# One even mixer rearranged: mLSTM sample tokens on partitions, new states on row halves, convolution taps in two chains

## The chip, the cores and the metric

One core of one Trainium2 chip. The time is device microseconds (us) of one launch, median of three runs. Engines: PE (TensorE matmul), PEld (its weight load), DVE (VectorE), ACT (ScalarE), POOL (GpSimd), SP (SyncE, which only issues DMAs here).

## The reference, cut to what matters

Two transformer layers run over 512 prompt tokens and 8 sequences of 8 sample tokens (64 "samples"), 576 tokens in all, D = 1024. Layer 0 has the even mixer, which is all that the change touches:

```python
def even_mixer(hn, state, W, j):
    a_val, a_gate, q, k, v, o, gates = split(hn @ W['ev_w_in'])
    u = a_val * sigmoid(a_gate)                      # 512 channels
    c = causal depthwise conv(u, 31 taps) + bias     # samples start from a stored history
    a_out = silu(layer_norm(c))                      # mean and variance over the channels
    li, lf = input gate, log_sigmoid(forget gate)    # 4 heads
    h, C1, n1, m1 = mlstm_scan(q, k * 128**-0.5, v, li, lf, C0, n0, m0)
    mix = concat(a_out, sigmoid(o) * h) @ W['ev_w_out']

# mlstm_scan, per head: s = (q k^T) * exp(decay - m);  den = sum(s) + w_inter * (q n0)
#   h = (s v + w_inter * (q C0)) / max(|den|, exp(-m));  C1 = decay * C0 + (w_s * k)^T v
```

For the prompt the old state is zero; each of the 8 sample sequences has its own C0 (128 x 128) and n0 per head. Before and behind the mixer stand SwiGLU blocks, a gated projection, and a second layer with attention.

## The kernel before, in words

**Products.** Channels lie on partitions and the 576 tokens on the free axis. A weight product is three matmuls (`mm3`, L642 to L644): the weight block `wr` rounded to fp32r, its remainder `wl`, and the same two parts of the input. A tile of 128 output channels takes 8 k-blocks x 2 token halves x 3 = 48 matmuls. Weights come in blocks of 2048 columns, two tiles of the mixer's input products or four of its output product. For each block SP loads `raw`, ACT rounds it to `wr` (L1218), POOL subtracts to make `wl` (L581), and PE then takes it. There are two such slots. PE's output goes to two PSUM banks, in turn banks 0-1 and 2-3, and the tile after next may start once DVE has emptied them.

**Even mixer, first half.** The products run in the order `glu` (4 blocks, 8 tiles: value and gate of u), the gate rows (48 + 48 narrow matmuls), `kv` (4 blocks) and `qo` (4 blocks). Beside them:
- DVE makes u (`up` for the prompt, `us` for the samples, L1905, L1906), then the 31 taps of 4 channel groups, one group at a time (`conv_chunk`, L1866; the accumulator is PSUM bank 6). Each tap waits for the one before. Chunks of 8 taps stand between the evacuations of tiles: three in `glu`, six in `kv`, seven in `qo`.
- POOL makes the sample products `prod` (`sample_taps`, L597, 8 instructions a group), DVE sums them (`sum_taps`, L1895). There is one `prod` buffer, so group j waits for the sum of group j - 1. POOL's order in `kv` is block, group 0, block, group 1, and so on (L614 to L619).
- After the gate rows DVE runs the row chain for decay and maximum (L1915 to L1949), with the evacuation of the first `kv` tile in its midst (`kT`, L1735).
- PE turns K and V (`turn`, L758) between tiles; ACT copies them out (L1342, L1344).

**Even mixer, second half (the tail).** PE spreads the rows of maxima (L796), forms the sum for the layer norm mean (L885), then of squares (L892). Then come the heads: for each, five units of scores (L808) and values (L823, L825; the samples' at L828, L829); DVE multiplies scores by decays that ACT made (`weigh`, L1979; `Ds`, L1416, L1419). `former` (L843, L845) is the old state's part for the samples: 8 matmuls of 8 columns with C0 as weights and one for n0. The denominator goes ACT Abs, DVE max, ACT Ln, ACT Exp, DVE multiply (L1487, L2025, L1491, L1493, L2033); that last step releases `states` on PE: 4 matmuls for the prompt (L854) and 8 of 64 rows for the samples (L858). DVE then makes the new states (`new_states`, L2050, L2054). The output product of the conv half (8 tiles of 24 matmuls, "conv pieces") is dealt out between heads:

```python
CONV_PIECES = {0: ((), ()), 1: ((0,), (1,)), 2: ((2,), (3,)), 3: ((4,), (5, 6, 7))}   # (before, after the states)
```

The order of ACT in the tail is written out by hand (from L1422): the copies `Mb`, the squares, then for each head decays, `kw` (L1477), at heads 1 and 3 the rounding of a weight block, the denominator steps, `xr` (L1495); behind head 0's, `conv_silu` (L1462 to L1466). After the last piece the output product of the mLSTM half (`out_mlstm`) starts.

Of the kernel before, what the change touches and what calls it, by code (L numbers as in the profile page):

```python
# [23 lines left out]
P = 128  # L24
# [28 lines left out]
CONST = dict(ident=128, cm=128, neg_incl=128, sb_neg=128, blk_ml=64, blk_col=8,  # L53
# [69 lines left out]
def build(nc, A):  # L123
# [94 lines left out]
    gcol = sb("gcol", [P, 2 * ST * HEADS], at=z)  # L218
# [3 lines left out]
    kwm = sb("kwm", [SMP, NB, P], at=z)  # L222
    smp = sb("smp", [P, HEADS, 3, SMP], at=z)
    wsm = sb("wsm", [SMP, NB], at=z)
    qn = tiny
    ENDS = [z[0]]
    Pm = [tg, sg]
    z = [ZONE]
# [62 lines left out]
    CONV_PIECES = {0: ((), ()), 1: ((0,), (1,)), 2: ((2,), (3,)), 3: ((4,), (5, 6, 7))}  # L291

    def rows_bank(hh):

        return 6 + hh % 2

    def floor_bank(hh):

        return 7 - hh % 2

    def state_banks(hh):
        return (4, 5, 7) if hh == HEADS - 1 else (NUM, DEN, rows_bank(hh))
# [268 lines left out]
    def _(e):  # L571
# [66 lines left out]
    def _(e):  # L638
# [110 lines left out]
        def turn(src, phase, t, n, bank=4):  # L749
# [12 lines left out]
        def turn_kv(n):  # L762
            turn(kT[:, n, :] if n < 4 else vtmp[n - 4][:], "kv", n, n)
# [5 lines left out]
        def turn_cols():  # L769
# [3 lines left out]
            for q, row in enumerate((rowa, rowws)):  # L773
                for i in range(ST):
# [3 lines left out]
                                     C("ident", 0, 4, rows=4))  # L778
            mm.then_inc(S("cols_turned"), 1)

        def spread_samples():

            e.wait_ge(S("cols_copied"), 4)
            for hh in range(HEADS):
# [3 lines left out]

        gemm("qo", xin(1), None, lambda t: turn_kv(6 + t) if t < 2 else turn_cols() if t == 2 else
             spread_samples() if t == 3 else None)  # L790

        e.wait_ge(S("cols_copied"), 6)
        for hh in range(HEADS):
            if hh == 2:
                e.wait_ge(S("tile_evacuated"), evac_at("qo", 7))
            e.matmul(ps[:, (4, 5, 2, 3)[hh], :], sel(hh), rowM[:, 0:SEQ], start=True, stop=True  # L796
                     ).then_inc(S("rows_spread"), 1)

        def scores(k):
# [6 lines left out]
            else:  # L806
                e.wait_ge(S("max_copied"), k + 1)
# [3 lines left out]
        def values(k):  # L811
            hh, i = divmod(k, ST)
            rws = rows_bank(hh)
# [13 lines left out]
            else:  # L827
                e.matmul(ps[:, rws, 0:SMP], vn[0:SMP, i, hh, 0:P], pm[0:SMP, 0:SMP], start=True, stop=True)  # L828
                e.matmul(ps[:, rws, SMP:2 * SMP], ones[0:SMP, :], pm[0:SMP, 0:SMP], start=True, stop=True  # L829
                         ).then_inc(S("pv_done"), 1)  # L830

        def floor(hh):

            e.matmul(ps[:, floor_bank(hh), :], sel(hh), rowem[:, 0:SEQ], start=True, stop=True
                     ).then_inc(S("floor_ready"), 1)

        def former(hh):

            rws = rows_bank(hh)
            e.wait_ge(S("qn_ready"), hh + 1)  # L840
            for b in range(NB):
                o = 2 * SMP + b * TB
                e.matmul(ps[:, rws, o:o + TB], C0[hh % 2][:, b, 0:P], qT[:, hh, SEQ + b * TB:SEQ + (b + 1) * TB],  # L843
                         start=True, stop=True)
            e.matmul(ps[:, rws, 3 * SMP:4 * SMP], ones[:], qn[:, 0:SMP], start=True, stop=True  # L845
                     ).then_inc(S("inter_ready"), 1)

        def states(hh):
            banks = state_banks(hh)
            e.wait_ge(S("kw_ready"), TM * (hh + 1))  # L850
            e.wait_ge(S("kwm_ready"), hh + 1)
            e.wait_ge(S("h_read"), hh + 1)
            for i in range(TM):
                e.matmul(ps[:, banks[2], 2 * (P + 1):3 * (P + 1)], kw[:, i, :], vn[:, i, hh, :],  # L854
                         start=i == 0, stop=i == TM - 1)
            for b in range(NB):
                o = (b % 3) * (P + 1)
                mm = e.matmul(ps[:, banks[b // 3], o:o + P + 1], kwm[:, b, :], vn[0:SMP, ST - 1, hh, :],  # L858
                              start=True, stop=True)
            mm.then_inc(S("state_ready"), 1)  # L860

        def conv_piece(t):
# [3 lines left out]
            if t == 0:  # L866
                e.wait_ge(S("conv_mixed"), TM)
# [13 lines left out]
        for j in range(TM):  # L881
            e.wait_ge(S("conv_done"), j + 1)
            e.wait_ge(S("taps_summed"), 2 * j + 2)
            for hf in range(2):
                mm = e.matmul(ps[:, hf, 0:HALF], ones[:], cv[:, j, hf * HALF:(hf + 1) * HALF],  # L885
                              start=j == 0, stop=j == TM - 1)
        mm.then_inc(S("ln_sum"), 1)
        e.wait_ge(S("ln_centered"), TM)
        for j in range(TM):
            e.wait_ge(S("ln_sq"), j + 1)  # L890
            for hf in range(2):
                mm = e.matmul(ps[:, hf, 0:HALF], ones[:], (hd, sq)[j % 2][:, hf * HALF:(hf + 1) * HALF],  # L892
                              start=j == 0, stop=j == TM - 1)
            mm.then_inc(S("ln_var"), 1)
        e.wait_ge(S("ones_ready"), 4)
        for hh in range(HEADS):
# [7 lines left out]
            if hh == 0:  # L904
                former(0)
            for t in behind:
                conv_piece(t)
            if hh < HEADS - 1:
                states(hh)
                former(hh + 1)  # L910
                for t in after_states:
                    conv_piece(t)
            else:
                conv_piece(after_states[0])
                states(hh)
                for t in after_states[1:]:
                    conv_piece(t)
# [282 lines left out]
    def _(e):  # L1200
# [139 lines left out]
        def copy_turned(n, full, part, bank=4):  # L1340
# [3 lines left out]
            e.activation(part, ps[0:SMP, bank + 1, 0:P], ACT.Copy).then_inc(S("turned_copied"), 1)  # L1344

        def copy_kv(n):
            dst = kn[:, :, n, :] if n < 4 else vn[:, :, n - 4, 0:P]
            copy_turned(n, dst[:, 0:TM, :], dst[0:SMP, TM, :])
# [22 lines left out]
        def copy_cols():  # L1371

            e.wait_ge(S("cols_turned"), 1)
            for q in range(2):
                o = q * ST * HEADS
                e.activation(gcol[:, o:o + 16], ps[:, 4, o:o + 16], ACT.Copy).then_inc(S("cols_copied"), 1)
                e.activation(gcol[0:SMP, o + 16:o + 20], ps[0:SMP, 4, o + 16:o + 20], ACT.Copy
                             ).then_inc(S("cols_copied"), 1)
            e.wait_ge(S("rows_spread"), 1)
# [5 lines left out]
        for n in blocks("qo"):  # L1385
# [15 lines left out]
        def decay(k):  # L1401
# [3 lines left out]
            if k >= 2:  # L1405
                e.wait_ge(S("p_ready"), k - 1)
            a = gcol[0:r, i * HEADS + hh:i * HEADS + hh + 1]
            if i == 0:
                e.wait_ge(S("masked"), hh + 2)
            if i == TM:  # L1410
                e.wait_ge(S("masked"), 1)
                e.activation(Ds[0:r, k % 2, 0:SMP], smpm[:, hh, :], ACT.Exp, scale=-1.0, bias=a
# [3 lines left out]
            e.activation(Ds[:, k % 2, 0:P], Md[:, hh, n0:n1], ACT.Exp, scale=-1.0, bias=a  # L1416
                         ).then_inc(S("decay_ready"), 1)
            if n1 < SEQ:
                e.activation(Ds[:, k % 2, P:SEQ - n0], Mb[:, hh, n1:SEQ], ACT.Exp, scale=-1.0, bias=a  # L1419
# [3 lines left out]
        for hh in range(HEADS):  # L1423
            e.wait_ge(S("rows_spread"), hh + 2)
            e.activation(Mb[:, hh, 0:SEQ], ps[:, (4, 5, 2, 3)[hh], :], ACT.Copy).then_inc(S("max_copied"), 1)
        decay(0)
        decay(1)
# [16 lines left out]
        for j in range(TM):  # L1444
            e.wait_ge(S("ln_centered"), j + 1)
            if j >= 2:
                e.wait_ge(S("ln_var"), j - 1)
            e.activation((hd, sq)[j % 2][:], cv[:, j, :], ACT.Square).then_inc(S("ln_sq"), 1)

        def conv_root():  # L1450

            e.wait_ge(S("ln_var"), TM)
            e.activation(two(acc[:]), unit(0), ACT.Ln, scale=1.0 / DA, bias=eps5[:, 0:1]
# [13 lines left out]

        for hh in range(HEADS):
            for i in range(2, ST):
                decay(ST * hh + i)  # L1470
            if hh:
                e.wait_ge(S("state_ready"), hh)
            else:
                conv_root()
# [4 lines left out]
            if hh == 1:  # L1479
# [4 lines left out]
            else:  # L1484
                next(out_conv)
            e.wait_ge(S("pv_done"), ST * (hh + 1))
            e.activation(tu[:, 0:SEQ], ps[:, DEN, :], ACT.Abs).then_inc(S("den_abs"), 1)  # L1487
            e.wait_ge(S("den_raw"), hh + 1)
            e.activation(tu[:, SEQ:T], tu[:, SEQ:T], ACT.Abs).then_inc(S("den_abs"), 1)
            e.wait_ge(S("den_ready"), 2 * hh + 2)  # L1490
            e.activation(tu[:], tu[:], ACT.Ln).then_inc(S("den_inverted"), 1)  # L1491
# [999 lines left out]
```

## Time and profile before

| | |
|---|---|
| median of 3 runs | 2637.61 us (2637.4 to 2640.54) |
| the profiled execution's own time | 2636.96 us |
| its span | 2635.1 us |
| mean granted PE clock | 0.978 of full |
| PE busy | 2539.5 us, 96% |
| PEld busy | 2431.6 us, 92% |
| DVE busy | 805.1 us, 31% |
| ACT busy | 757.4 us, 29% |
| POOL busy | 836.6 us, 32% |

The even mixer's first half runs from 447.8 to 627.3 us of the span, its tail from 627.3 to 763.9 us. Busy shares are means over stages with different limits; the granted clock is a share of 2.4 GHz, 0.5 is the lower level of 1.2 GHz.

### The profile page before, as it was taken

What the parts mean: (1) busy time and instruction counts of PE and PEld (TensorE: products, weight loads), DVE (VectorE), ACT (ScalarE), POOL (GpSimd) and SP (SyncE); (2) the same over time, 40 slices, a digit from 0 to 9 for tenths busy, and PEclk for the clock granted to TensorE, in tenths of its full rate; (3) what the DMA queues carried; (4) which work ended last, traced back from release to release, by engine and by line L of the source; (5) the groups of instructions that cost most, each with busy time, mean ns of one, the idle gap of its engine ahead of it and who ended that gap; (6) DMA issues with size and microseconds to landing.
All of it is one profiled execution on the core that took longest, in us unless ns stands there. A gap on an engine that the chain in (4) does not pass through costs nothing.

```text
span 2635.1 us, 43853 instructions
## 1 busy us (share of the span) xinstructions
PE 2539.5 (96%) x18378; PEld 2431.6 (92%) x18378; DVE 805.1 (31%) x1227; ACT 757.4 (29%) x903; POOL 836.6 (32%) x247
## 2 busy tenths in 40 slices
PE   7999999989899999999999999999997999999997
PEld 7999999987689999999999999997774799999997
DVE  3220222686552211224322022212225522102233
ACT  4221223213423222224322122312233432212243
POOL 3333324452023333333433333431110133333332
PEclk9999999999799999999999999999998999999998
DMA  4222223411112222222222221232124122222222
GB/s 153 80 81 91 84 71 102 88 65 65 51 67 80 76 72 92 81 78 80 90 89 71 96 80 67 97 130 81 63 88 152 56 81 80 76 100 80 75 73 72
DMA packets 67829, 220.84 MB, mean 84 GB/s; under 512 B 13895, under 2 KB 33223, under 8 KB 52107
## 3 DMA queue, kind: packets, MB, share of 16 engines
q1 hardware_dynamic: 51104, 200.61, 22.3%
q10 hardware_dynamic: 16618, 18.70, 2.6%
q8 instruction: 82, 1.34, 0.2%
q14 instruction: 25, 0.20, 0.0%
HBM read 207.95 MB, written 11.33 MB: 83 GB/s over the span
## 4 chain that ended last, share of the span: by engine, by line
issue 52%; POOL 10%; PE 9%; ACT 1%; DVE 0%; POOLq 0%; DVEq 0%; ACTq 0%
POOL wl L581 10%; PE ps L642 2%; PE ps L643 2%; PE ps L644 2%; PE ps L1025 1%; PE ps L982 0%; PE ps L1040 0%; POOLq L633 0%; PE ps L985 0%; DVE h L2331 0%; ACT wr L1218 0%; PE ps L843 0%; PE ps L702 0%; PE ps L1065 0%; PE ps L858 0%
## 5 line engine op out<-in xcount | busy, mean ns | idle before, releaser
L581 POOL TENSOR_TENSOR wl<-raw,wr 128x2048 fp32r<-128x2048 f32 (+3 forms) x206 | 810.1, 3934 | 1724.7 <-ACT wr L1218 1724.7
L642 PE MATMUL ps<-xr,wr 128*128 128x288 f32 x4096 | 1220.3, 298 | 39.3 <-POOL wl L581 31.7
L643 PE MATMUL ps<-xl,wr 128*128 128x288 f32 x4096 | 1214.3, 296 | 0.0
L644 PE MATMUL ps<-xr,wl 128*128 128x288 f32 x4096 | 1211.9, 296 | 0.0
L642 PEld LDWEIGHTS ps<-xr,wr 128*128 128x128 f32 x4096 | 775.2, 189 | 46.4 <-issue 24.3
L643 PEld LDWEIGHTS ps<-xl,wr 128*128 128x128 f32 x4096 | 775.7, 189 | 1.1
L644 PEld LDWEIGHTS ps<-xr,wl 128*128 128x128 f32 x4096 | 776.1, 189 | 0.0
L1218 ACT ACTIVATE wr<-raw 128x2048 fp32r<-128x2048 f32 (+1 forms) x200 | 351.9, 1759 | 305.4 <-PE ps L644 270.7
L643 PE MATMUL ps<-hl,wr 128*128 128x288 f32 x1408 | 415.4, 295 | 0.0
L644 PE MATMUL ps<-hr,wl 128*128 128x288 f32 x1408 | 415.0, 295 | 0.0
L642 PE MATMUL ps<-hr,wr 128*128 128x288 f32 x1408 | 413.1, 293 | 0.0
L642 PEld LDWEIGHTS ps<-hr,wr 128*128 128x128 f32 x1408 | 264.7, 188 | 0.9 <-issue 0.9
L643 PEld LDWEIGHTS ps<-hl,wr 128*128 128x128 f32 x1408 | 264.7, 188 | 0.0
L644 PEld LDWEIGHTS ps<-hr,wl 128*128 128x128 f32 x1408 | 264.5, 188 | 0.0
L1273 ACT ACTIVATE hr<-hd 128x576 f32 (+1 forms) x88 | 60.4, 687 | 571.3 <-DVE hd L1749 571.3
L1733 DVE TENSOR_TENSOR tu<-ps,R 128x576 f32<-128x576 f32 x96 | 72.7, 758 | 493.5 <-PE ps L644 493.5
L1733 DVE TENSOR_TENSOR tg<-ps,R 128x576 f32<-128x576 f32 x111 | 84.1, 758 | 335.6 <-PE ps L644 309.5
L1762 DVE SCALAR_TENSOR_TENSOR h<-ps,h 128x576 f32 x64 | 48.5, 758 | 411.6 <-PE ps L644 411.6
L1270 ACT ACTIVATE sg<-tg 128x576 f32<-128x576 f32 x88 | 60.5, 687 | 253.0 <-DVE tg L1733 253.0
L1249 ACT ACTIVATE xr<-h,prm 128x576 fp32r<-128x576 f32 (+1 forms) x64 | 49.7, 777 | 231.9 <-DVE h L1762 167.0
L1753 DVE TENSOR_TENSOR hl<-hd,hr 128x576 f32 x88 | 66.8, 759 | 91.3 <-ACT hr L1273 91.3
L1866 DVE SCALAR_TENSOR_TENSOR ps<-up,prm,ps 128x512 f32<-128x512 f32 x116 | 87.6, 755 | 18.6 <-DVE ps L1866 17.0
(338 smaller groups left out, 1414.4 us busy)
## 6 DMA issues: line engine op xcount, KB each, us to landing
raw<-in_up SPq DMA_DIRECT2D x88, 1024.0 KB, 4.8
raw<-in_down SPq DMA_DIRECT2D x32, 768.0 KB, 4.3
raw<-in_mixin SPq DMA_DIRECT2D x24, 1024.0 KB, 4.8
raw<-in_down SPq DMA_DIRECT2D x32, 640.0 KB, 3.9
raw<-in_ple SPq DMA_DIRECT2D x16, 640.0 KB, 3.8
raw<-in_mixout SPq DMA_DIRECT2D x8, 1024.0 KB, 4.8
kring<-in_kc SPq DMA_DIRECT2D x16, 256.0 KB, 4.3
vring<-in_vc SPq DMA_DIRECT2D x16, 256.0 KB, 3.1
```

What stands on the lines that cost most here:

```text
L581: ins = e.tensor_tensor(wl[s][:, c], raw[s][:, c], wr[s][:, c].bitcast(F32), ALU.subtract)
L642: e.matmul(out, wrt, xrt, start=first, stop=False)
L643: e.matmul(out, wrt, xlt, start=False, stop=False)
L644: return e.matmul(out, wlt, xrt, start=False, stop=last)
L1218: e.activation(wr[slot][:, 0:w], raw[slot][:, 0:w], ACT.Copy).then_inc(S("w_rounded"), 1)
L1249: e.activation(xj, hj, ACT.Copy, scale=prm[:, bass.ds(j + g0, 1)]).then_inc(S("xr_ready"), 1)
L1270: e.activation(sg[:], tg[:], ACT.Silu).then_inc(S("silu_ready"), 1)
L1273: e.activation(hr[:, bass.ds(i * 2 + s, 1), :].rearrange("p a t -> p (a t)"), hd[:], ACT.Copy).then_inc(S("hr_ready"), 1)
L1733: ins = e.tensor_tensor(two(out), unit(u), two(R[:]), ALU.mult)
L1753: e.tensor_tensor(q, hd[:], r.bitcast(F32), ALU.subtract).then_inc(S("hidden_ready"), 1)
L1762: e.scalar_tensor_tensor(hj, unit(s), 0.5, hj, ALU.mult, ALU.add).then_inc(S("tile_evacuated"), 1)
L1866: ins = e.scalar_tensor_tensor(out, inp, w, accp, ALU.mult, ALU.add)
```

## The change

- **Taps.** Two channel groups are convolved side by side, with accumulators in PSUM banks 6 and 7; a tap waits for the tap before the last. They stand at other places: none after the first pair of `glu` tiles, 10, 10 and 12 instructions after the next three, 8 after each of `kv` tiles 2 to 7 and `qo` tiles 0 to 4, 4 after `qo` tile 5.
- **Sample taps.** POOL makes group j - 1 behind `glu` block j, group 3 behind `kv` block 0. DVE sums group j - 1 behind the taps of `glu` pair j.
- **Layer norm.** PE forms the mean's sum between `qo` tiles 6 and 7 (banks 4, 5), DVE centers at once, ACT squares into four buffers behind the sigmoid of tile 6, and the squares are summed right behind the spread rows.
- **Samples in the heads.** Sample tokens lie on output partitions: `former` is 8 accumulating matmuls of 129 columns whose weights are q x w_inter of one sequence, zero elsewhere (`qm`), with the old state as moving data; the score part (64 x 129) is added to the same region. DVE makes the 64 x 1 denominator (4 small instructions), scales the rows, PE turns them (one transpose).
- **New states.** K and V of the samples are also put on partitions 64 to 127 (one more matmul in each `turn`, and two in the turning of the columns); the 8 state matmuls go in turn to rows 0-63 and 64-127 and to different banks. Seven stand ahead of the prompt's four, the last behind, with a wait on the first seven.
- **Order.** ACT's decays have two buffers for units 0 and 1. `conv_silu` moves ahead of head 0's `kw` and denominator, the weight roundings to heads 0 and 2, and piece 0 behind head 0's states.

```diff
-    CONV_PIECES = {0: ((), ()), 1: ((0,), (1,)), 2: ((2,), (3,)), 3: ((4,), (5, 6, 7))}
+    ROWS, FLOOR = 6, 7
+    CONV_PIECES = {0: ((), (0,)), 1: ((1,), (2,)), 2: ((3,), (4,)), 3: ((5,), (6, 7))}
+    CONV_TAPS = {("glu", 1): 5, ("glu", 2): 5, ("glu", 3): 6,
+                 **{("kv", t): 4 for t in range(2, 8)}, **{("qo", t): 4 for t in range(5)}, ("qo", 5): 2}
...
     @block.gpsimd
-            if name == "kv":
+            if name in ("glu", "kv"):
                 for n in range(4):
                     low_part(p, n // 2, n % 2)
-                    sample_taps(n)
+                    if name == "glu" and n:
+                        sample_taps(n - 1)
+                    if (name, n) == ("kv", 0):
+                        sample_taps(TM - 1)
...
     @block.tensor
+            if twice:
+                mm = e.matmul(ps[SMP:P, bank + 1, 0:P], src[:, SEQ:T], C("ident"), start=True, stop=True)
...
         def former(hh):
+            e.wait_ge(S("qm_ready"), hh + 1)
+            e.wait_ge(S(f"C0_loaded{hh % 2}"), 16 * (hh // 2 + 1))
             for b in range(NB):
+                mm = e.matmul(rows_of(hh)[0], qm[:, b * SMP:(b + 1) * SMP], C0[hh % 2][:, b, :],
+                              start=b == 0, stop=False)
...
         def states(hh):
+            def own(b):
+                r = slice(b % 2 * SMP, (b % 2 + 1) * SMP)
+                return e.matmul(state_of(hh, b), kwm[r, b // 2, :], vn[r, ST - 1, hh, :], start=True, stop=True)
+            for b in range(NB - 2):
+                own(b)
+            own(NB - 2).then_inc(S("state_ready"), 1)
             for i in range(TM):
+                e.matmul(ps[:, FLOOR, o:o + P + 1], kw[:, i, :], vn[:, i, hh, :],
                          start=i == 0, stop=i == TM - 1)
+            e.wait_ge(S("state_ready"), 2 * hh + 1)
+            own(NB - 1).then_inc(S("state_ready"), 1)
...
+            turn_samples(hh)
+            states(hh)
             if hh < HEADS - 1:
-                states(hh)
                 former(hh + 1)
-                for t in after_states:
-                    conv_piece(t)
+            for t in after_states:
+                conv_piece(t)
...
     @block.scalar
+        for i in range(2):
+            decay(i)
+        conv_root()
+        for i in range(2, ST):
+            decay(i)
+        conv_silu()
         for hh in range(HEADS):
...
-            if hh == 1:
+            if hh == 0:
                 next(out_conv)
...
+            if hh == HEADS - 2:
                 next(out_conv)
...
     @block.vector
+    with e.Fori(0, done) as i:
+        for q in range(2):
+            tap(2 * pair + q, i + k, wait=i * 2 + (base + q - 1))
...
-            if j < TM - 1:
-                conv_chunk(j)
+            conv_taps(CONV_TAPS.get(("glu", j), 0))
+            if j:
+                sum_taps(j - 1)
...
+        e.wait_ge(S("ln_root"), 2)
+        for j in range(TM):
+            e.tensor_tensor(cv[:, j, :], cv[:, j, :], acc[:], ALU.mult).then_inc(S("ln_scaled"), 1)
         weigh(0)
         weigh(1)
...
         def output(hh, behind):
+            e.wait_ge(S("den_abs"), hh + 1)
+            e.wait_ge(S("floor_ready"), hh + 1)
+            e.tensor_tensor(tu[:, 0:SEQ], ps[:, FLOOR, :], tu[:, 0:SEQ], ALU.max).then_inc(S("den_ready"), 1)
+            sample_rows(hh)
```

## Rows read from the trace of the kernel before

**Rows 1.** Windows by stage: window, length, PE, PEld, DVE, ACT, POOL busy, PEclk, DMA, GB/s.

```profile
447.80:506.40 58.60, 58.60 (x437) 57.39 (x437) 29.71 (x45) 15.42 (x14) 23.58 (x12) 1.00 0.38 109
506.40:570.80 64.40, 57.26 (x416) 56.45 (x414) 53.41 (x72) 17.64 (x24) 33.83 (x28) 0.95 0.37 55
570.80:627.30 56.50, 56.47 (x412) 55.76 (x412) 47.94 (x65) 12.25 (x18) 19.17 (x5) 0.97 0.23 79
627.30:652.10 24.80, 18.54 (x46) 10.30 (x45) 9.78 (x15) 9.22 (x17) 4.94 (x4) 0.79 0.20 78
652.10:677.50 25.40, 21.21 (x94) 16.13 (x92) 12.52 (x33) 15.07 (x26) 0.00 (x0) 0.72 0.02 5
677.50:709.10 31.60, 28.05 (x123) 22.33 (x124) 13.89 (x30) 10.05 (x22) 4.59 (x1) 0.74 0.30 102
709.10:736.10 27.00, 25.46 (x125) 20.78 (x124) 11.14 (x29) 7.01 (x17) 0.00 (x0) 0.81 0.06 23
736.10:763.90 27.80, 23.94 (x149) 19.77 (x148) 15.28 (x29) 6.98 (x12) 4.58 (x1) 1.00 0.11 39
```

**Rows 2.** Waits, 447 to 770 us: who waited for whom, total, times, longest.

```profile
POOL prod L597 <- DVE cv L1895: 27.8, 3, 9.9
...
PE ps L642 <- POOL wl L581: 7.2, 3, 5.0
```

**Rows 3.** Timeline of POOL in `glu`: start, duration, instruction, idle before and releaser.

```profile
478.06 4.62 POOL L581 TENSOR_TENSOR wl<-raw,wr 128x2048 fp32r<-128x2048 f32 x1 [8.17 <-ACT wr L1218]
...
495.45 5.14 POOL L597 TENSOR_TENSOR prod<-us,prm 128x248 f32<-128x248 f32 x8
```

**Rows 4.** Timeline of DVE: taps, an evacuation between taps, and the sum.

```profile
477.40 0.76 DVE L1866 SCALAR_TENSOR_TENSOR ps<-up,prm,ps 128x512 f32<-128x512 f32 x1 [0.36 <-DVE us L1906]
...
549.26 0.75 DVE L1866 SCALAR_TENSOR_TENSOR ps<-up,prm,ps 128x512 f32<-128x512 f32 x1 [0.18 <-DVE ps L1866]
550.20 0.76 DVE L1866 SCALAR_TENSOR_TENSOR ps<-up,prm,ps 128x512 f32<-128x512 f32 x1 [0.18 <-DVE ps L1866]
550.86 0.75 DVE L1733 TENSOR_TENSOR sq<-ps,R 128x576 f32<-128x576 f32 x1
551.53 0.75 DVE L1866 SCALAR_TENSOR_TENSOR ps<-up,prm,ps 128x512 f32<-128x512 f32 x1
...
558.73 2.21 DVE L1895 TENSOR_REDUCE cv<-prod 128x64 f32<-128x1984 f32 x1
```

**Rows 5.** Timeline of DVE: first step of the gate rows, and the first `kv` evacuation.

```profile
506.68 0.74 DVE L1915 TENSOR_TENSOR rowa<-ps,R 4x576 f32<-4x576 f32 x1 [4.04 <-PE ps L644]
...
515.81 0.76 DVE L1735 SCALAR_TENSOR_TENSOR kT<-ps,R 128x576 f32<-128x576 f32 x1
```

**Rows 6.** Timeline of POOL and of DVE at 686 us: two that overlap.

```profile
686.49 4.59 POOL L581 TENSOR_TENSOR wl<-raw,wr 128x2048 fp32r<-128x2048 f32 x1 [46.18 <-ACT wr L1218]
...
688.67 2.48 DVE L1992 TENSOR_TENSOR tiny<-qT,C 128x64 f32<-128x64 f32 x1
```

**Rows 7.** Timeline of ACT: `conv_silu`, its first activation and the table load behind it.

```profile
670.68 0.87 ACT L1462 ACTIVATE cv<-cv,prm 128x576 f32<-128x576 f32 x1
...
676.70 1.28 ACT L1466 ACT_TABLE_LOAD   x1
```

**Rows 8.** Timeline of PE; each fp32 matmul leaves two records.

```profile
650.03 1.13 PE L892 MATMUL ps<-hd,ones 128*128 128x288 f32 x4
...
722.99 1.13 PE L854 MATMUL ps<-vn,hd 128*128 128x129 f32 x8 [1.54 <-DVE acc L2033]
724.05 3.19 PE L858 MATMUL ps<-vn,kwm 64*128 64x129 f32 x16
727.17 3.58 PE L843 MATMUL ps<-qT,C 128*128 128x8 f32 x16
...
753.24 2.05 PE L858 MATMUL ps<-vn,kwm 64*128 64x129 f32 x16
...
1841.63 0.49 PE L982 MATMUL ps<-oq,ok 64*128 64x128 f32 x4
```

More of the change, by code:

```diff
@@ L778, in turn_cols @@
                                      C("ident", 0, 4, rows=4))
+                mm = e.matmul(ps[SMP:P, 4, o:o + HEADS], row[:, SEQ:T], C("ident", 0, 4, rows=4),
+                              start=True, stop=True)
+            o = 2 * ST * HEADS
+            mm = e.transpose(ps[0:SMP, 4, o:o + HEADS], rowem[:, SEQ:T], C("ident", 0, 4, rows=4))
             mm.then_inc(S("cols_turned"), 1)
         def spread_samples():
-            e.wait_ge(S("cols_copied"), 4)
+            e.wait_ge(S("cols_copied"), 5)
             for hh in range(HEADS):
@@ L880, in _ @@
         scores(1)
[L881 to L894, printed above, removed]
         e.wait_ge(S("ones_ready"), 4)
+        former(0)
         for hh in range(HEADS):
@@ L1339, in _, with copy_turned @@
             e.dma_start(A["conv_s"][:, j], us[:, j, :, TB:TB + HIST]).then_inc(S("conv_stored"), 16)
-        def copy_turned(n, full, part, bank=4):
+        def copy_turned(n, full, part, bank=4, rows=SMP):
             e.wait_ge(S("turned"), n + 1)
@@ L1396, in _ @@
                     e.activation(oT[:, o, :], tu[:], ACT.Sigmoid).then_inc(S("o_ready"), 1)
+                    if o == 2:
+                        for j in range(TM):
+                            e.wait_ge(S("ln_centered"), j + 1)
+                            e.activation(squares[j][:], cv[:, j, :], ACT.Square).then_inc(S("ln_sq"), 1)
         e.preload_act_table_set("natural_log_exp_and_others")
@@ L1410, in decay @@
             if i == TM:
-                e.wait_ge(S("masked"), 1)
-                e.activation(Ds[0:r, k % 2, 0:SMP], smpm[:, hh, :], ACT.Exp, scale=-1.0, bias=a
+                e.activation(dst[0:r, :], smpm[:, hh, :], ACT.Exp, scale=-1.0, bias=a
                              ).then_inc(S("decay_ready"), 1)
@@ L1443, in _ @@
         load_state(1)
[L1444 to L1448, printed above, removed]
         def conv_root():
-            e.wait_ge(S("ln_var"), TM)
-            e.activation(two(acc[:]), unit(0), ACT.Ln, scale=1.0 / DA, bias=eps5[:, 0:1]
+            e.wait_ge(S("ln_var"), 1)
+            e.activation(two(acc[:]), unit(3), ACT.Ln, scale=1.0 / DA, bias=eps5[:, 0:1]
                          ).then_inc(S("ln_root"), 1)
@@ L1869, in conv_chunk @@
[L1869 to L1889 removed]
+            e.wait_ge(S("conv_step"), wait)
@@ new lines, in conv_taps @@
+        def conv_taps(n):
+            while n:
+                pair, k = divmod(conv_at[0], TAPS)
+                done = 1
+                if k == 0:
+                    first_tap(2 * pair)
+                    first_tap(2 * pair + 1)
+                elif k == TAPS - 1:
+                    last_tap(2 * pair)
+                    last_tap(2 * pair + 1)
+                else:
+                    done = min(n, TAPS - 1 - k)
+                    base = 2 * (pair * (TAPS - 1) + k)
+                    with e.Fori(0, done) as i:
+                        for q in range(2):
+                            tap(2 * pair + q, i + k, wait=i * 2 + (base + q - 1))
+                conv_at[0] += done
+                n -= done
@@ L1967, in _ @@
                 normed(tu[:], t % 2, done_at("qo", t))
-            if t < 7:
-                conv_chunk(9 + t)
+            conv_taps(CONV_TAPS.get(("qo", t), 0))
+            if t == 6:
+                e.wait_ge(S("ln_sum"), 1)
+                for j in range(TM):
+                    e.scalar_tensor_tensor(two(cv[:, j, :]), psn, -1.0 / DA, two(cv[:, j, :]), ALU.mult, ALU.add
+                                           ).then_inc(S("ln_centered"), 1)
         def weigh(k):
@@ L2085, in _ @@
                                     ).then_inc(S("conv_mixed"), 1)
-            for t in after_states[hh == HEADS - 1:]:
+            new_states(hh)
+            for t in after_states:
                 take_conv_piece(t)
```

306 lines of the change are left out of this document (149 added, 157 removed).

## The prediction, made before the changed kernel ran

> **What bounds the kernel now.** I read the windows by stage first [rows 1]. The first half of the mixer (447.8 to 627.3 us) is bound by PE at full clock, except in `kv`, where PE is busy 57.3 of 64.4 us. The tail (627.3 to 763.9 us) is bound by a chain that crosses engines: PE is idle or at 0.72 to 0.81 of its clock in four of five windows. The waits then name the holes [rows 2]: PE waited 7.2 us for `wl`, because POOL stood in `sample_taps` until DVE had summed the group before. Everything outside these 316 us is untouched.
>
> **Part 1, a tap.** A tap that waits for its forerunner starts 0.94 us after it; one behind an unrelated instruction starts 0.67 us after that [rows 4]. In the new loop a tap's forerunner is two back, done 0.6 us earlier, so I take 0.67. Bounds: 0.67, and 0.94 if register work in the loop, not the result, sets the pace; between the evacuation and the next tap the loop was even set up anew within 0.67, which is why I take the lower. With 124 taps that is 32 us of DVE time, but DVE's time is on the path at a few places only.
> One rule speaks against it. The Trainium skill, VectorE: DVE Perf Modes, section The DRAIN you can't avoid, says that the next instruction waits for the pipe to empty whether or not a semaphore stands between. The 0.67 against 0.94 above does not agree; by the rule alone two chains would gain nothing (rival C has the time, from rows).
>
> **Part 2, `glu`.** What is late now is POOL's third remainder. Before, block 3's was made at 478.1 to 482.7, long before PE wanted it at 487.4 [rows 3]. Now it stands behind group 1's products, and these behind DVE's sum of group 0, which stands behind 10 taps. DVE: u at 477.0 and taps from 477.4, as now, 10 x 0.67 and 0.2 for the first two to 484.3, sum 2.2 to 486.5 [rows 4]. POOL: products 5.1 [rows 3], 0.8 for two DVE instructions let in between (part 3), remainder 4.6, to 497.1. PE has meanwhile been late by 0.3 for block 2 (behind group 0's products), so it wants block 3 at 487.7 and waits 9.3. Its clock then is low for some us; from the PEclk column the existing three waits lost some 3.5 us in `kv` and `qo` (0.05 x 64.4 + 0.03 x 56.5 = 4.9, some of it idle time) [rows 1], so 2.0 for a long one. `kv` starts 0.3 + 9.3 + 2.0 = 11.6 us late, at 518.
>
> **Part 3, start of `kv`.** `glu` tile 7 ends at 511.7. DVE: evacuation, sigmoid, u to 514.1; 12 taps to 522.6; sum and bias to 525.1. Only then does the row chain start, which takes 9.1 us to the first `kv` evacuation [rows 5]: 534.2. POOL: group 3's products 525 to 530, block 1's remainder to 535. The two get in each other's way: a DVE instruction with two SBUF inputs that starts during a POOL instruction ends only with it (688.67 + 2.48 = 691.15 beside 686.49 + 4.59 = 691.08) [rows 6]. The scan in the row chain is one such, so it ends at 536.7 and the evacuation at 537.4. PE wanted block 1, and with it banks 0-1, at 518 + 12.8 = 530.8: 6.6 us wait, 2.0 of clock. Bounds: 534.5 without the collision; 542.5 if POOL's next remainder comes in ahead of the scan. So `kv` block 1 and what follows is 11.6 + 8.6 = 20.2 us late.
>
> **Part 4, rest of the first half.** The 7.2 us of waits and some 3.4 of clock go (POOL has only remainders left, DVE needs 0.67 + 8 x 0.67 = 6.0 us a tile against PE's 6.4 to 7.0): -10.6. Added: 8 turnings x 0.22 (128 columns at the rate of [rows 8], 0.48 for 288) = 1.8; 8 matmuls of the mean 3.8, moved here from the tail. `qo` ends at 627.3 + 20.2 - 10.6 + 5.6 = 642.5, say 642: **15 us later**. ACT's stores of the conv state (4 us of issue) and its rounding of `kv` block 1 end by 521, ahead of POOL's 530. The memset of `qm` and the moved centering and squares lie beside other work (PE's tile 7 for the last two). SP's loads follow the remainders and have 5 us or more to spare each.
>
> **Part 5, tail up to head 0** (times from the end of `qo`). Spread rows 4 x 0.86 and squares 8 x 0.48 (both from 0.48 per 288 columns) [rows 8]: 7.4, with no 3.4 us wait for the late last evacuation and so at full clock. ACT root 1.5, DVE scaling 4 x 0.67 and first `weigh` 0.7: values start at 12.4, before at 24.8 [rows 1]. Scores and `former` (8 x 0.26; C0 lands at about 9.8, since its load still waits for `Mb`) fit in between. If the low-row spread matmuls make the clock fall, 16.
>
> **Part 6, head 0.** Units take 8.4 as before. But ACT now has `conv_silu` first: decays to 10.2, table 1.3, silu and copies 6.0, table 1.3 [rows 7], `kw` 1.2, the rounding 1.9, decays for head 1 1.6: 23.5, Abs to 24.1. POOL's remainder (22.0 to 26.6) then holds DVE's `qm` multiplication for head 1 (two SBUF inputs, the case of [rows 6]), which stands ahead of the max. Max 27.4, Ln, Exp, multiply 29.5. PE idles 7.5 us from 20.9 on, and does states, `former` and piece 0 at half clock for the most part: 12 x 0.46 + 0.5 for the turn and the new wait, 8 x 0.43, 4.8 = 14.2. Head 0 ends at 43.7: 31.3 us, before 25.4 without a piece.
>
> **Part 7, heads 1 to 3.** `former` before: 3.6 + 0.5 at half clock; now 3.5. States: before 4.3 of 12 matmuls [rows 8]. On row halves I take a pair at 0.49, as the two matmuls of 64 rows at 1841.63, against 2.05 / 4 = 0.51 at 753.24: 0.1 us a head, less than the new wait before the last one and the transpose cost (0.5). Bounds: nothing, and half of the 2.05.
> The Trainium skill, TensorEngine Tiling (Array Packing), section Theoretical Speedup, gives up to 2 x for 64 rows; by it the eight would save 1.0 at full clock in each head, an estimate, 4 us in all.
> The denominator chain loses Abs and max of the samples but still waits for the second `weigh` and the piece's evacuation: PE idles 1.4, as at 722.99 [rows 8]. So heads 1 and 2 take 8.4 + 3.4 + 1.4 + 13.1 = 26.3 each, before 31.6 and 27.0; head 1 loses the 2.2 us collision and 2.1 of wait with it. Head 3 has three pieces, not four, and no POOL collision: 7.1 + 3.3 + 1.4 + 3.3 + 3.3 + 1.0 + 3.3 + 0.8 = 23.5, before 27.8. The rounding at head 2 delays `xr` by 3 us and the new states with it, to about when head 3 wants the banks; hidden by `former` and piece 4, 2 us if not.
> Tail: 12.4 + 31.3 + 26.3 + 26.3 + 23.5 = 119.8, before 136.6: **17 us shorter**.
>
> **Sum.** +15 - 17 = -2 us. The profiled execution took 2636.96, so 2635.0; the median is 0.65 above it: 2635.5 us.
>
> **Rivals.** A, faster (0.34): the clock holds in the tail. New `former` streams 129 columns, where the old spent 0.45 us on a weight load for 8 columns; head 3's states ran at full clock (2.05 against 3.19) [rows 8]. Full clock in two heads saves 4.3 each, and if the scan slips past POOL another 3: 2624 to 2629. Against: dense fp32 work in the window from 627.3 did not bring the clock back (0.79).
> B, slower through `glu` and `kv` (0.12): POOL's remainder gets in before the scan (+5) and the clock falls in the spread rows (+3.6), or the new states of head 2 hold head 3 (+2): 2641 to 2646. It decides if the scan starts after 535.3.
> C, slower through the taps (0.10): 0.94 a tap. `glu` +2.7, row chain +3.2, and in `kv` and `qo` 8.2 us of DVE per tile against 6.4 to 7.0: the mean would wait until about 650, some 17 us late: 2652. Against: 0.67 in rows 4.
> That the change doesn't do what it says I exclude for the stalls, which follow from program order.
>
> **How the numbers follow.** A measurement of this kernel tells 0.2%, 5.3 us, from no change. My forecast's own case, within 5.3 us, has 0.44. Range: bounds -3 (no collision) and -8 (clock) from the forecast, +5 and +3.6 above, and C in part: 2624 to 2648. Faster 0.34, same 0.44, slower 0.22.
>
> **What would show it.** Right: taps 0.67 apart; a PE wait of 8 to 10 us for `wl` before `glu` block 3 near 488 and one of 5 to 8 near 531; none for `wl` after that; `qo` ending near 642; values of head 0 12 to 13 us behind it; an idle of 7 us before head 0's states; the tail near 120. Wrong: `kv` starting before 510 (POOL is not held), taps at 0.9, PEclk at 1.0 in heads 1 and 2 (A), or head 0 without its wait.

## The result, and the profile after

The changed kernel takes 2651.95 us (median of 5 runs, 2651.04 to 2655.43) against 2637.61: ratio 1.0055, 95% interval 1.0043 to 1.0066. **Slower by 14 us**, where 2635.5 with a range of 2624 to 2648 was forecast. The profiled execution spans 2650.1 us, 15.0 more than before. Ratios of the experiments below are taken to runs of the kernel before made beside them, with medians of 2637.5 us (e1 to e4), 2639.3 (e5 to e8) and 2637.7 (e9 to e12).

The windows by stage, as in [rows 1] (`glu` with the gate rows, seven of the eight `kv` tiles, the rest to the end of `qo`, the start of the tail, heads 0 to 3):

```profile
449.06:518.30 69.24, 60.66 (x437) 59.01 (x437) 34.82 (x52) 15.41 (x14) 34.22 (x28) 0.95 0.29 90
518.30:593.00 74.70, 68.07 (x489) 65.28 (x488) 66.53 (x88) 19.28 (x26) 29.96 (x13) 0.95 0.31 64
593.00:645.20 52.20, 52.20 (x378) 50.25 (x377) 35.45 (x53) 13.57 (x21) 14.55 (x4) 1.00 0.24 82
645.20:661.42 16.22, 14.60 (x46) 8.57 (x45) 5.24 (x10) 10.64 (x19) 4.93 (x4) 0.79 0.18 65
661.42:687.75 26.33, 18.93 (x96) 13.50 (x97) 13.62 (x29) 15.13 (x29) 4.51 (x1) 0.87 0.16 58
687.75:709.15 21.40, 20.06 (x121) 15.03 (x120) 10.51 (x28) 5.96 (x16) 0.00 (x0) 1.00 0.14 45
709.15:731.23 22.08, 20.21 (x121) 14.94 (x119) 14.27 (x29) 7.63 (x16) 4.54 (x1) 1.00 0.19 61
731.23:754.73 23.50, 20.39 (x124) 15.96 (x124) 10.60 (x27) 4.58 (x9) 0.00 (x0) 1.00 0.13 49
```

The mixer ends at 754.73 us, before at 763.9: the edited stages are **faster** by 9.2 us, by 10.4 if one counts that they begin 1.2 us later (449.06, before 447.84). The first half ends 18 us later (`qo` at 645.2, before at 627.3), the tail takes 109.5 us where it took 136.6. So some 24 us are lost behind the mixer, in code that the diff does not touch. The same evacuation of the next SwiGLU block, and of the last stage, in the timeline of DVE, before:

```profile
800.79 0.76 DVE L1733 TENSOR_TENSOR tg<-ps,R 128x576 f32<-128x576 f32 x1 [4.50 <-ACT R L1257]
...
2591.49 0.76 DVE L1733 TENSOR_TENSOR tg<-ps,R 128x576 f32<-128x576 f32 x1 [3.27 <-PE ps L644]
```

and after:

```profile
791.64 0.76 DVE L1775 TENSOR_TENSOR tg<-ps,R 128x576 f32<-128x576 f32 x1 [4.56 <-ACT R L1298]
...
2606.50 0.76 DVE L1775 TENSOR_TENSOR tg<-ps,R 128x576 f32<-128x576 f32 x1 [3.25 <-PE ps L663]
```

9.15 us early becomes 15.0 us late. In the windows below it is not a wait that grew: PE is busy for the whole of each at full clock, and only fits fewer matmuls into it. Windows of PE alone, before (length, busy, count, PEclk, DMA, GB/s):

```profile
60.00:160.00 100.00, 100.00 (x752) 1.00 0.21 72
185.00:235.00 50.00, 50.00 (x380) 1.00 0.30 100
820.00:920.00 100.00, 100.00 (x759) 1.00 0.23 81
1300.00:1400.00 100.00, 100.00 (x758) 1.00 0.24 84
```

and after:

```profile
60.00:160.00 100.00, 100.00 (x752) 1.00 0.20 73
185.00:235.00 50.00, 50.00 (x377) 1.00 0.30 100
820.00:920.00 100.00, 100.00 (x746) 1.00 0.22 79
1300.00:1400.00 100.00, 100.00 (x746) 1.00 0.24 84
```

The first window (up products of the first block, moving data `xr`) is the same in both. In the others (moving data `hr`, `hl`, `xr2`, `xl2`) the counts drop. From the start times in the trace a matmul of 288 columns follows the one before by one of three values, steady through a stage: 133.3 ns with `xr`; elsewhere 132.2 before, and 134.4 after (133.3 in the down products of the first block). Three later blocks of 3168 matmuls (44 tiles of 48 and 2 x 8 of 72 or 60) by 2.2 ns are 21.1 us of the 24.2; 1056 down products of the first by 1.1 ns are the 1.2 us of the late start. Of the remaining 3.1 us, 2.0 arise in the odd mixer and the rest between the first two of these blocks, at 1224 to 1234 us, where the changed kernel's granted clock is 0.83 and that of the kernel before 1.00. e1 below, with the zone where it was, loses 1.5 us at the same place, so this part is not the address.

What the diff does to these stages is one number, on a line that the cut diff ahead of the prediction leaves out: the mask `blk_col` shrinks from 8 to 4 columns. With it the table `cst` shrinks by 16 bytes a partition, and its buffer (rounded up to a multiple of 32) by 32. Everything allocated behind it moves down by 32 bytes, also the part of SBUF that I call the zone, which holds `hr`, `hl`, `xr2` and `xl2`. Counted from the weight buffers and modulo 128 bytes, `xr` lies at 0 in both kernels, the zone at 64 before and at 32 after.

### The profile page after: what moved, and what is told of

Read it like the earlier page. It is cut to its first block, busy times and chain, and to the rows that moved or that the text cites. A ratio compares the mean times of both kernels' runs of the same rounds, so it can differ in the third digit from the quotient of the medians.

```text
span 2650.1 us, 43855 instructions
## 1 busy us (share of the span) xinstructions
PE 2550.9 (96%) x18387; PEld 2440.7 (92%) x18387; DVE 802.4 (30%) x1224; ACT 755.4 (29%) x900; POOL 836.1 (32%) x247
## 4 chain that ended last, share of the span: by engine, by line
issue 53%; PE 32%; POOL 11%; DVE 2%; ACT 1%; POOLq 0%; DMA 0%; DVEq 0%; SPq 0%; ACTq 0%
POOL wl L597 11%; PE ps L661 9%; PE ps L663 9%; PE ps L662 9%; PE ps L1066 1%; PE ps L1023 0%; ACT wr L1259 0%; DMA raw<-in_up 0%; PE ps L845 0%; PE ps L777 0%; PE ps L1081 0%; PE ps L858 0%; POOL prod L613 0%; DVE rowB L1985 0%; POOLq L652 0%
## 5 line engine op out<-in xcount | busy, mean ns | idle before, releaser
L1750 DVE SCALAR_TENSOR_TENSOR xl<-h,prm,xr 128x576 fp32r<-128x576 f32 (+1 forms) x64 | 61.8, 966 | 70.4 <-ACT xr L1290 70.4
```

What stands on the lines that cost most here:

```text
L1750: e.scalar_tensor_tensor(lj, hj, prm[:, bass.ds(j + (POFF["gains"] + m * KD), 1)], xj.bitcast(F32), ALU.mult, ALU.subtract).then_inc(S("x_ ...
```

## Experiments

**Does the address do it?** Three runs move the zone of the changed kernel, one that of the kernel before.

```diff
+    top[0] += 32          # e1; 96 in e3, 64 in e4
     ZONE = top[0]
```
```diff
-    eps6 = sb("eps6", [P, 1])
-    eps5 = sb("eps5", [P, 1])
+    eps = sb("eps6", [P, 2])      # e2, in the kernel before: one 32-byte cell fewer
+    eps6, eps5 = eps[:, 0:1], eps[:, 1:2]
```

Expected of the 32 bytes: 

> The changed kernel with 32 unused bytes a partition ahead of the zone that holds hr, hl, xr2 and xl2, so that these stand again where they stood before the change (blk_col 8 to 4 had moved them 32 bytes down). Address theory: the products of the three later SwiGLU blocks go back from 134.4 to 132.2 ns a matmul, 9504 x 2.2 ns = 21 us, and the down products of the first from 133.3 to 132.2, 1 us: 2651.95 - 22 = 2630 us, ratio 0.997 to before. Program theory (the pitch comes from the instruction stream or from the clock's history, which the pad doesn't touch): 2652, pitch 134.4.

Expected of the kernel before with its zone 32 bytes lower: 

> The kernel before, with eps6 and eps5 in one 32-byte cell, so that the zone stands 32 bytes lower, as in the changed kernel; no instruction differs but for addresses. Address theory: 134.4 ns in the products of SwiGLU blocks 1 to 3, 133.3 in the first one's down products, 2637.6 + 22 = 2660 us, ratio 1.0085. Program theory: 2637.6, 132.2 ns.

Expected of 96 bytes: 

> The changed kernel with 96 bytes ahead of the zone, which puts it on the same residue of 128 bytes as xr and xl. Address theory: all products at the 133.3 ns that those with xr show, 9504 x 1.1 ns = 10.5 us less than the changed kernel: 2641 us. Program theory: 2652.

Expected of 64 bytes: 

> The changed kernel with 64 bytes ahead of the zone (residue 96 of 128). Address theory: a pitch other than 134.4 ns is likely; if only the odd multiple of 32 counts, 134.4 and 2652 again, if the order of the four residues counts, between 132.2 and 134.4 and 2630 to 2652. Program theory: 2652.

| run | zone from the weights, mod 128 | ns, `xr` stages | ns, zone stages | median us (runs) | ratio to before, interval |
|---|---|---|---|---|---|
| before | 64 | 133.3 | 132.2 | 2637.5 (23) | |
| changed | 32 | 133.3 | 134.4 | 2651.95 (5) | 1.0055 (1.0043 to 1.0066) |
| e1 | 64 | 133.3 | 132.2 | 2632.55 (12) | 0.9978 (0.9967 to 0.9990) |
| e2 | 32 | 133.3 | 134.4 | 2654.7 (5) | 1.0063 (1.0050 to 1.0077) |
| e3 | 0 | 133.3 | 133.3 | 2641.8 (10) | 1.0019 (1.0007 to 1.0031) |
| e4 | 96 | 133.3 | 132.2 | 2630.2 (4) | 0.9963 (0.9948 to 0.9977) |

The window of PE at 820 us (before x759, changed x746), of e1:

```profile
820.00:920.00 100.00, 100.00 (x759) 1.00 0.21 77
```

and of e2:

```profile
820.00:920.00 100.00, 100.00 (x746) 1.00 0.22 76
```

The address theory had the pitches of e1, e2 and e3 right (of e4 it said only that 134.4 was unlikely), and the program theory fell: e2 changes nothing but the addresses behind one cell, and the kernel before becomes as slow as the changed one. In medians e1 gained 19 us and e2 lost 17, 22 expected of both. Runs of one kernel differ by up to 17 us here, in step with their mean clock (0.985 in e1's run of 2625.6 us, 0.978 in that of 2642.1), and 9 of the 12 runs of e1 have a lower one than the 0.984 of most runs of the changed kernel. At the same mean clock of 0.984, e1's run of 2626.2 us stands 25 us below the changed kernel's of 2651.0 to 2652.0. With the zone where it was, the rearranged mixer alone is worth 0.2% less time, 5 us by medians. e1's traced run is one of its fastest, and there the span is 10.7 us shorter than before; what the clock did in its slower runs, no trace shows.

**Whose address counts?** e5 puts 64 bytes ahead of `xr`, so that inputs, weights and zone all move (weights and `xr` at residue 64, zone 96). e6 allocates the weights ahead of `xr`, and the 64 bytes between them.

```diff
     h = sb("h", [P, KD, T])
+    top[0] += 64                # e5; in e6 behind raw, wr and wl, which stand here, not behind xl
     XR_AT = top[0]
```

Expected of e5: 

> The changed kernel with 64 bytes ahead of xr: the inputs xr and xl and the weights behind them at residue 64 of 128 bytes, the zone at 96. If the residue of the moving data alone sets the pitch, the products with xr (up products of the first SwiGLU block, and the mixers) go from 133.3 to 132.2 ns, 2112 + some 2000 matmuls, 4 to 5 us less than with 64 bytes ahead of the zone alone (2630.2): 2626. If it is the distance between moving data and weights, those stay at 133.3 and the zone, now 32 from the weights, goes back to 134.4: 2652. If both count, something else.

Expected of e6: 

> The changed kernel with the weight buffers ahead of xr, and 64 bytes between: weights at residue 0, xr and xl at 64, the zone at 96. Moving data alone, or the distance to the weights: both say 132.2 ns everywhere, 2626 us; beside the run with the weights at 64 it tells the two apart.

Measured: e5 2651.97 us, ratio 1.0059 (1.0040 to 1.0078); e6 2624.0 us, 0.9952 (0.9936 to 0.9967). The same PE windows, of e5:

```profile
60.00:160.00 100.00, 100.00 (x753) 1.00 0.21 73
...
820.00:920.00 100.00, 100.00 (x746) 1.00 0.21 77
1300.00:1400.00 100.00, 100.00 (x753) 1.00 0.24 84
```

and of e6:

```profile
60.00:160.00 100.00, 100.00 (x758) 1.00 0.22 77
...
820.00:920.00 100.00, 100.00 (x758) 1.00 0.22 79
```

Moving data have the same residues in both (64 and 96), only the weights differ (64 and 0). So it is the **distance** between moving data and weights: 0 gives 133.3 ns, 64 and 96 give 132.2, and 32 gives 134.4. Distance 32 also shows 133.3 in some stages (the down products of the first block, and in e5 the block at 1300 us); what decides between the two is open. That the distance counts modulo 128 bytes rests on these few placements, all multiples of 32 bytes. In e6 even the `xr` stages run at 132.2, for the first time.

The Trainium skill, SBUF — State Buffer, section Operand start alignment, says that an operand must start at a multiple of its element size, and that this is about legality, the runs behind it having timed nothing. All addresses here are legal by it; the 2.2 ns are what it leaves open.

**Do the row halves overlap, and do they hold the clock?** e7 is e1 with the sample states in another order.

```diff
-            for b in range(NB - 2):
+            for b in (0, 2, 4, 1, 3, 5):
                 own(b)
```

Expected: 

> The changed kernel with 32 bytes ahead of the zone, and the seven sample states in the order 0, 2, 4, 1, 3, 5, 6, so that only two neighbours lie on different row halves. If neighbours on different halves overlap, the seven take 1.7 to 1.8 us (0.256 each, from 2.05 for eight in the kernel before) in place of 1.13, 0.6 a head, 2.4 in all, the clock held: 2630 + 2.4. If the overlapping is also what holds the clock in the heads, the granted clock falls to a half in heads 1 and 2 and each costs 4 more: 2638 to 2642. If the order doesn't matter, 1.13 again.

Measured: 2630.7 us (one run), heads 1 and 2 at clock 1.00. In the lines, x14 are the seven sample states, x2 the eighth, x8 the four of the prompt and x16 `former`, since each fp32 matmul leaves two records. Timeline of PE in head 1, e7:

```profile
700.64 1.24 PE L910 MATMUL ps<-vn,kwm 64*128 64x129 f32 x14 [1.33 <-DVE acc L2092]
701.81 1.16 PE L917 MATMUL ps<-vn,hd 128*128 128x129 f32 x8
```

and of the changed kernel:

```profile
701.38 1.13 PE L909 MATMUL ps<-vn,kwm 64*128 64x129 f32 x14 [1.34 <-DVE acc L2091]
702.44 1.16 PE L916 MATMUL ps<-vn,hd 128*128 128x129 f32 x8
703.53 0.49 PE L909 MATMUL ps<-vn,kwm 64*128 64x129 f32 x2
703.94 1.99 PE L894 MATMUL ps<-C,qm 128*64 128x129 f32 x16
```

Seven in 1.13 us, where the kernel before took 2.05 for eight on one half [rows 8]: they do overlap. But 1.24 in the blocked order was neither value expected. The start times in the trace show why: the records fall into two trains, each 0.11 us apart, as those of the one train in the kernel before are, and the upper half's begins 0.30 us behind the lower one's, when the third of the lower half's three matmuls has not begun. The seventh, whose record carries the semaphore, starts its last record at 701.50 us, ahead of the last record of the sixth at 701.61. So PE let matmuls of one half pass those of the other. Since they overlapped in this order too, the run does not tell whether the overlap is what holds the clock. All on one half was not tried in this kernel.

**Are the narrow matmuls what took the clock down?** e9 is e1 with the old `former`'s eight matmuls of 8 columns added in heads 1 to 3; e10 is the kernel before with seven of the eight left out there.

```diff
+            for b in range(NB if hh else 0):                                  # e9
+                e.matmul(ps[:, ROWS, o:o + TB], C0[hh % 2][:, b, 0:P], qT[:, hh, SEQ + b * TB:SEQ + (b + 1) * TB], ...)
```
```diff
-            for b in range(NB):                                               # e10, in the kernel before
+            for b in range(NB if hh == 0 else 1):
```

Expected of e9: 

> The changed kernel with 32 bytes ahead of the zone, and eight more matmuls with C0 as weights and 8 moving columns (those of the kernel before, output unused) at the start of each former of heads 1 to 3. If such narrow matmuls, which load 128 columns of weights for 8 of data, are what took the clock down in the heads before: the granted clock is a half behind the states of heads 1 and 2, as before, and each of the three heads that get them is 3 to 6 us longer, 2630 + 12 = 2642. If not, only their own time at full clock, some 1.8 us in each of three, 2636, and heads 1 and 2 at 1.0.

Expected of e10: 

> The kernel before, which leaves out seven of the eight narrow C0 matmuls of former in heads 1 to 3 (so the old state's part of seven sample sequences is missing there). If they take the clock down, it holds in heads 1 and 2 (no half-clock stretch near 694 and 725 us) and each head's states and former shrink from 11.4 and 8.1 us at half clock to some 4: 2637.5 less 3 x 3.1 and 2 x 3 for the clock, 2622. If they don't, the clock falls at the states as before, and only the 3.1 us of the narrow matmuls themselves go in three heads: 2628.

Measured: e9 2638.7 us, e10 2626.0 (one run each). Windows of PE, e9, heads 1 and 2:

```profile
689.42:712.69 23.27, 21.93 (x138) 1.00 0.18 63
712.69:735.97 23.28, 21.94 (x138) 1.00 0.13 44
```

and e10, heads 0 to 2:

```profile
654.54:678.32 23.78, 18.19 (x79) 0.75 0.00 1
678.32:704.79 26.47, 24.93 (x108) 0.78 0.25 85
704.79:725.41 20.62, 19.08 (x111) 1.00 0.16 56
```

Added to the changed kernel they cost their own 1.9 us a head and the clock stays. Left out of the kernel before, head 2 holds the clock and shrinks from 27.0 to 20.6 us. Head 1 shrinks from 31.6 to 26.5, but the low clock of head 0 reaches into it (0.78), which was not expected. Both kinds of head do the same in other traces: e2, whose instructions are those of the kernel before, is at half clock in heads 1 and 2 as that kernel is, and in none of the traces with the new heads (changed, e1, e3 to e9, e11, e12) does the clock fall there. So without the narrow matmuls it held in head 2, but they alone don't bring it down. What about the new head keeps it up stays **open**.

**Can the waits of the first half be had back?** e8 is e1 with

```diff
+    CONV_TAPS = {("glu", 1): 5, ("glu", 2): 6, **{("kv", t): 5 for t in range(2, 7)}, ("kv", 7): 4, ...   # qo as it was
...
-                    if name == "glu" and n: sample_taps(n - 1)
-                    if (name, n) == ("kv", 0): sample_taps(TM - 1)
+                    for j in {("glu", 1): (0,), ("glu", 3): (1, 2), ("kv", 1): (3,)}.get((name, n), ()):
+                        sample_taps(j)
...
+            if j: sum_taps(j - 1)
             conv_taps(CONV_TAPS.get(("glu", j), 0))
-            if j: sum_taps(j - 1)
```

Expected: 

> The changed kernel with 32 bytes ahead of the zone; DVE sums group j - 1 ahead of the taps, POOL makes group 0 behind glu block 1, groups 1 and 2 behind block 3, group 3 behind kv block 1; no taps behind the last glu pair (12 moved to kv tiles, 10 a tile). Queue theory: the 8.4 us wait before glu block 3 goes, and the one of 6.6 before kv block 1 with it (the row chain starts right behind the gate rows, first kv evacuation near 516), and some 3 us of half clock: 18 us less, qo ends near 628, 2614 us. Rival: ten taps and an evacuation are 7.5 us of DVE against PE's 7.5 a tile in kv, so PE now waits for banks in each kv tile, some 1 us each, and half of it is given back: 2622. Second rival: the waits are not POOL's doing, and nothing moves: 2632.

Measured: 2620.15 us, ratio 0.9931 (0.9916 to 0.9947). Waits of PE, 440 to 640 us:

```profile
PE ps L660 <- DVE kT L1776: 3.0, 1, 3.0
PE ps L660 <- DVE tg L1774: 2.5, 1, 2.5
```

Against the changed kernel's, 447 to 760 us:

```profile
PE ps L661 <- POOL wl L597: 8.6, 2, 8.4
PE ps L661 <- DVE kT L1777: 6.6, 1, 6.6
PE ps L901 <- DVE hrow L2077: 6.4, 1, 6.4
PE ps L909 <- DVE acc L2091: 5.0, 4, 1.3
```

POOL's wait is gone; DVE's shrank and a new one came (an evacuation behind ten taps). The time is nearer to the first rival's 2622 than to the 2614 of the queue theory, but not for its reason: its waits in each `kv` tile did not come, 7.5 us of DVE fit into 7.5. What is missing are the two waits above, 5.5 us of the 15 that were to go.

**The version that beats both.** e11 mends those two (4 taps, not 10, behind the second `glu` pair; the second `kv` evacuation ahead of the last row steps) and takes e6's order of buffers. e12 adds to it (besides the lines shown, DVE makes the low parts of the conv inputs behind head 1's units):

```diff
-        conv_silu()                       # ACT, ahead of head 0
...
             e.activation(xr[:, TM + hh, :], sq[:], ACT.Copy).then_inc(S("mixr_ready"), 1)
+            if hh == 0: conv_silu()
...
-    CONV_PIECES = {0: ((), (0,)), 1: ((1,), (2,)), ...
+    CONV_PIECES = {0: ((), ()), 1: ((0,), (1, 2)), ...
```

Expected of e11: 

> The early sums with the two waits that they left mended (4 taps, not 10, behind the second glu pair, so that tile 4 is evacuated in time; the second kv tile evacuated ahead of the last row steps; 10 taps behind kv tile 7 and qo tile 5), and the weights ahead of xr with 64 bytes between. Queue theory: the 2.5 us wait at 490 and the 3.0 us at 534 and up to 3.4 of half clock go from the early sums' 2620, and the alignment takes another 5 (4096 matmuls by 1.1 ns): 2609 to 2612. Rival: DVE, now at 7.4 of 7.5 us a kv tile, makes PE wait for banks and gives the 5 us back: 2616.

Expected of e12: 

> The same, and conv_silu moved from ahead of head 0's keys to behind its denominators and its xr, the low parts of the conv inputs behind head 1's units, piece 0 from head 0 to head 1. If ACT's silu chain is what PE waits for in head 0 (the idle of 6.4 us ahead of hrow): most of it goes, 5 us less than the kernel without this move, and head 0 is 17 to 18 us rather than 26. Rival: PE waits for the silu chain and the low parts ahead of piece 0 in head 1 instead, and 2 to 4 of the 5 are given back.

Measured: e11 2606.3 us, ratio 0.9881 (0.9864 to 0.9897), 3 us below the 2609 to 2612 expected; e12 **2601.1 us, ratio 0.9860 (0.9843 to 0.9876)**, 36 us less than before and 51 less than the changed kernel. Waits of PE in e12, 440 to 740 us:

```profile
PE ps L908 <- DVE acc L2094: 5.1, 4, 1.3
PE ps L660 <- DVE h L2064: 2.7, 3, 0.9
PE ps L900 <- DVE hrow L2080: 2.2, 1, 2.2
```

Both waits of the first half are gone, and of the 6.4 us ahead of head 0's `hrow` 2.2 are left. Head 0 takes 20.2 us, where it took 26.3 with piece 0 in it, and not the 17 to 18 expected: its clock is still at half in part (0.83 in the mean).

## Why the prediction was wrong

**The step that failed** is the last sentence of its opening paragraph on what bounds the kernel, "Everything outside these 316 us is untouched", which put the rest of the program at nothing. The rest cost 25 us: 21 in the later blocks and 1 in the first one's down products, both by the slower pitch that e1 and e2 trace to the 32 bytes, and 3 beside it (2.0 in the odd mixer, not settled, and a clock fall near 1230 us that e1 has too). The full diff names the step in the line for `blk_col`; I took it for a mask's width, not for the address of all that is allocated behind. Without this term the forecast of 2635.5 stands against e1's 2632.55, inside its range, but this is in part luck: it holds errors of both signs, as the points below show. It is luck too that rival C named 2652, the time that was measured: its reason, slow taps, did not come.

Point by point, from the timeline of the changed kernel:

```profile
479.73 5.36 DVE L1906 SCALAR_TENSOR_TENSOR ps<-up,prm,ps 128x512 f32<-128x512 f32 x8
...
487.35 5.64 POOL L613 TENSOR_TENSOR prod<-us,prm 128x248 f32<-128x248 f32 x8 [11.35 <-DVE cv L1947]
492.96 4.50 POOL L597 TENSOR_TENSOR wl<-raw,wr 128x2048 fp32r<-128x2048 f32 x1
497.51 0.61 PE L661 MATMUL ps<-xr,wr 128*128 128x288 f32 x1 [8.40 <-POOL wl L597]
...
530.73 10.58 POOL L597 TENSOR_TENSOR wl<-raw,wr 128x2048 fp32r<-128x2048 f32 x2
531.40 5.55 DVE L1985 TENSOR_TENSOR_SCAN rowB<-rows,rowt 4x576 f32<-4x576 f32 x1
536.99 0.76 DVE L1777 SCALAR_TENSOR_TENSOR kT<-ps,R 128x576 f32<-128x576 f32 x1
537.89 0.58 PE L661 MATMUL ps<-xr,wr 128*128 128x288 f32 x1 [6.63 <-DVE kT L1777]
```

- **Taps** (part 1): 0.67 us, eight in 5.36. Right; rival C fell.
- **`glu`** (part 2): a wait of 9.3 and `kv` from 518 were forecast; 8.4 and 518.3 came. Right; the stage began 1.2 us late, which the shorter wait makes up for the most part.
- **Start of `kv`** (part 3): a wait of 6.6, the scan held to 536.7, the evacuation over at 537.4; 6.63, 536.95 and 537.75 came. Right, and the collision is how it came about: the scan, 1.72 us in e8 beside POOL's short `prod` instructions, took 5.55 beside POOL's remainder, the first of the two in the line above (530.73 to 535.75), and ended 1.2 us behind it. The Trainium skill, SBUF — State Buffer, section SBUF: two separate sides, calls the pair of ports that VectorE and GpSimd share an exclusive lock for a whole instruction; the trace agrees. Rival B, by which the remainder gets in ahead of the scan, fell: the scan started at 531.4.
- **Rest of the first half** (part 4): `qo` was to end at 642 and ended at 645.2. `kv` began 0.3 us behind the forecast (part 2). The turnings were mis-sized: a tile with its turning takes 7.49 us (553.72 to 561.21), before 6.94 (578.85 to 585.79), so the matmul to the upper partitions costs 0.55 and not 0.22: 2.6 us over eight.
- **Up to head 0** (part 5): 16.2 us, not 12.4. It is the case named there as "16" and, with 3.6 us, in rival B: the clock fell in the spread rows (0.79 in the window from 645.20). The sum had left it out.
- **Head 0** (part 6): the idle was forecast at 7.5 us (the times given there, 20.9 to 29.5, make it 8.6); 6.4 and 1.0 came. But 26.3 us, not 31.3: states, `former` and piece 0, put at 14.2 us "at half clock for the most part", took 9.6, since the clock came back in the states (0.80 from 678.16 to 687.75).
- **Heads 1 to 3** (part 7): 21.4, 22.1 and 23.5 us, forecast 26.3, 26.3 and 23.5. This is the second term that was mis-sized, and it is **rival A**: the clock held. Heads 1 and 2 are 4.9 and 4.2 us shorter than forecast, 0.3 of which the row halves gave (seven in 1.13 and one in 0.49 are 0.4 less than the 2.05 before, where 0.1 had been taken). The Trainium skill, TensorEngine Tiling (Array Packing), section Theoretical Speedup, has up to twice the rate for 64 rows, by which I had estimated 1.0 a head. The seven come part of the way (1.13 against 7/8 of 2.05, 1.79, so 1.6 times), and the eighth, which waits for them, gives a part back.
- **Sum of the mixer**: +15 - 17 = -2 forecast, +18 - 27 = -9 measured: the first half 3 us longer than forecast (the turnings above all), the tail 10 shorter (heads 0 to 2 by 5.0, 4.9 and 4.2 for the clock above all, less the 3.8 of part 5).

## What to carry to other kernels

Read a diff for what it does to addresses: a table or pad that changes size shifts every buffer behind it, and here 32 bytes changed the pace of 10,560 matmuls by 0.8 to 1.7%, more than the whole rearrangement was worth. Where one part of a program gets faster and the whole slower, count matmuls in equal windows of a stage that was not edited, before looking for waits. If PE bounds the kernel, measure the few distances between moving data and weights and fix the best one by an explicit pad, so that later edits compare on equal ground.

## What the runs showed of the hardware that I had not expected

- The pitch of fp32r matmuls of 288 columns depends on the distance of the two SBUF operands modulo 128 bytes: 133.3 ns at 0, 134.4 (in some stages 133.3) at 32, 132.2 at 64 and at 96. Other widths and types, and distances that are not multiples of 32, were not tried.
- Matmuls of 64 rows on different row halves overlap even when they are issued in blocks of three (seven in 1.24 us against 1.13 interleaved), and a later one on one half starts ahead of an earlier one on the other. So in e7 the semaphore on the seventh says nothing of the sixth, whose last record starts 0.11 us later; in the changed kernel's order the seventh starts last (702.24, the sixth 702.05).
- A TENSOR_SCALAR with one tensor in SBUF and a column of scalars (the bias behind a sample sum, 0.25 us elsewhere) was held by POOL too: 3.40 us from 479.55 us in e8, to the end of the remainder at 482.9.
- Whether PE keeps its clock through a head is not a matter of one instruction: the narrow matmuls of the old `former` had to go from the kernel before for it to hold in head 2, and could be added to the new kernel without it falling.
